# Expert down matrices loaded in pairs, 64 partitions to an expert, and multiplied on 64-row tiles: a two-layer decoder trunk on one core

## The reference

```python
for i in range(DEPTH):                      # 2 layers, 256 tokens, width 1024
    ...                                     # convolution, linear attention, latent attention, merged
    x = layer_norm(alpha * x + mix, ...)
    # mixture of experts: 8 groups of 8, best group, then its two best experts
    y = 0
    for each token t, for each of its two experts e:
        h = silu(x[t] @ w_gate[e]) * (x[t] @ w_up[e])      # 1024 -> 256
        y[t] += weight[t, e] * (h @ w_down[e])             # 256 -> 1024
    x = layer_norm(alpha * x + y, ...)
    ple = sigmoid(x @ w_ple_gate + b) * (p[i] @ w_ple_up)
    x = layer_norm(alpha * x + ple, ...)
```

## Time and profile before

| | |
|---|---|
| median of 3 runs | 1505.33 us (1503.81 to 1505.48) |
| profiled execution, its own time | 1503.91 us |
| its span | 1502.2 us |
| PE busy | 1259.2 us (84%) |
| DVE, ACT, POOL busy | 554.2, 207.2, 27.9 us |
| DMA moved | 503.85 MB, mean 335 GB/s |
| granted TensorE clock, mean | 0.924 of 2.4 GHz |

### The profile page before, as it was taken

One profiled execution on the slowest core, in us unless ns is written; L12 is line 12 of the kernel. 1 busy time (PEld: TensorE's weight loads), 2 busy tenths in 40 slices (PEclk: granted clock), 3 DMA queues, 4 the chain that ended last, 5 costly groups with the idle time before them and its releaser, 6 DMA issues.

```text
span 1502.2 us, 20998 instructions
## 1 busy us (share of the span) xinstructions
PE 1259.2 (84%) x8621; PEld 690.0 (46%) x8621; DVE 554.2 (37%) x987; ACT 207.2 (14%) x413; POOL 27.9 (2%) x90
## 2 busy tenths in 40 slices
PE   9999999986774777579999999999677568757797
PEld 5665444742342434235466554456334325423354
DVE  6677775510110111111667677754111101101126
ACT  2322000310100000000212220012111000000011
POOL 2000000000000000000100000000000000000000
PEclk9999999997888889889999999999888879888899
DMA  9644558899999999999955255679999999999992
GB/s 314 230 172 150 174 211 332 318 426 426 427 427 425 425 425 426 428 427 416 330 192 204 97 204 168 230 301 355 426 427 426 427 426 424 426 426 428 426 408 87
DMA packets 110537, 503.85 MB, mean 335 GB/s; under 512 B 13042, under 2 KB 16132, under 8 KB 62468
## 3 DMA queue, kind: packets, MB, share of 16 engines
q1 hardware_dynamic: 109876, 501.84, 83.3%
q10 hardware_dynamic: 592, 1.06, 0.2%
HBM read 501.83 MB, written 1.05 MB: 335 GB/s over the span
## 4 chain that ended last, share of the span: by engine, by line
PE 60%; DMA 36%; issue 1%; SPq 1%; DVE 1%; ACT 0%; POOL 0%; DVEq 0%; POOLq 0%
DMA scratch<-in_w_down 35%; PE ps L852 20%; PE ps L1497 11%; PE ps L901 6%; PE ps L1448 5%; PE ps L805 4%; PE ps L1429 2%; PE ps L1507 2%; PE ps L1615 1%; PE ps L1344 1%; PE ps L825 1%; SPq L553 1%; PE ps L1316 0%; DMA ring<-in_w_in 0%; PE ps L1367 0%
## 5 line engine op out<-in xcount | busy, mean ns | idle before, releaser
L1497 PE MATMUL ps<-ring,pads 128*32 128x512 f32 x384 | 161.6, 784 | 199.2 <-DMA scratch<-in_w_down 199.2
L1497 PEld LDWEIGHTS ps<-ring,pads 128*32 128x32 f32 x384 | 33.9, 139 | 300.6 <-DMA scratch<-in_w_down 162.3
L1448 PE MATMUL ps<-scratch,pads 128*32 128x256 f32 x1792 | 171.6, 379 | 0.0
L1448 PE MATMUL ps<-ring,pads 128*32 128x256 f32 x2304 | 171.4, 379 | 0.0
L852 PE MATMUL ps<-ring,scratch 128*128 128x512 f32 x384 | 169.2, 592 | 0.0
L1497 PE MATMUL ps<-scratch,pads 128*32 128x512 f32 x512 | 161.6, 790 | 0.0
L2657 DVE COPY mats<-ps 128x512 f32<-128x512 f32 x32 | 22.1, 691 | 349.3 <-PE ps L1497 349.3
L1429 PEld LDWEIGHTS ps<-pads,xT 128*128 128x128 f32 x960 | 114.8, 197 | 25.3 <-issue 25.3
L1429 PE MATMUL ps<-pads,xT 128*128 128x128 f32 x960 | 116.0, 280 | 10.6 <-issue 10.6
L1507 PE MATMUL ps<-mats,pads 128*128 128x512 f32 x256 | 118.8, 606 | 0.0
L1448 PEld LDWEIGHTS ps<-scratch,pads 128*32 128x32 f32 x1792 | 89.3, 110 | 58.9 <-issue 17.6
(11 more groups left out here) (364 smaller groups left out, 1314.3 us busy)
## 6 DMA issues: line engine op xcount, KB each, us to landing
ring<-in_w_up SPq DMA_DIRECT2D x28, 2048.0 KB, 32.5
scratch<-in_w_down SPq DMA_DIRECT2D x28, 2048.0 KB, 23.0
scratch<-in_w_gate SPq DMA_DIRECT2D x28, 2048.0 KB, 30.4
ring<-in_w_in SPq DMA_DIRECT2D x48, 1024.0 KB, 7.1
ring<-in_w_gate SPq DMA_DIRECT2D x12, 3072.0 KB, 31.8
scratch<-in_w_up SPq DMA_DIRECT2D x14, 2048.0 KB, 31.9
ring<-in_w_down SPq DMA_DIRECT2D x14, 2048.0 KB, 27.0
scratch<-in_w_gate SPq DMA_DIRECT2D x22, 1024.0 KB, 14.5
```

What stands on the lines that cost most here:

```text
L1448: ins = mm(ps[32 * j:32 * j + 32, 2, i * 256:i * 256 + 256], xgT[:, k, 32 * j:32 * j + 32], w[j][:, k, :], start=(k == 0), stop=(k == K - 1))
L1497: ins = mm(ps[32 * j:32 * j + 32, n, :], hT[:, cc, 32 * j:32 * j + 32], w[j][:, cc, n * 512:n * 512 + 512], start=(cc == 0), stop=(cc == 1 ...
```

## The change

- **Slots.** `w_down` of experts 0 and 1 of a turn, and of 2 and 3, now need two neighbouring slots. The ring and `x` become one tensor `ring_x`, in which `x` follows `r[11]`, and the order of slots in each layer is shifted so that the pairs are neighbours. In scratch memory the pair is EARLY+4 and EARLY+5; LATE, which was in it before, takes the gate matrix of expert 0 of the even turns, which was in EARLY+5.
- **Loads.** `load_down`: two experts are 512 rows of w_down; they are laid on 128 partitions with four neighbouring rows in each, 16 KB in one piece, so that the first expert has partitions 0 to 63 and the second 64 to 127. Where matrices are loaded singly (turn 0, half of turn 1), a load brings one half of the 16 KB of all partitions. The last turn keeps the layout of before.
- **Products.** The down product of an expert is four matmuls of 64 rows for each half of the columns, 32 matmuls in a turn. Experts 0 and 2 lie on rows 0 to 63 of the array, 1 and 3 on 64 to 127. For this `gate_up` puts the experts into strips in the order 0, 2, 1, 3 (`place_of`), the hidden values are taken in quarters (`hquarter`) and transposed by eight 64 x 64 products with the identity, and `weigh_P` permutes its columns in the same way.
- **Counting.** `ring_free` rises at other instructions for the down slots, since reads of a pair end together.

```diff
-    for end in (4, 8, 10, 12):
+    for end in (4, 8):
...
+    for n in (8, 10):
+        assert slots[n + 1] - slots[n] == 1 or (slots[n], slots[n + 1]) == (RING - 1, XSLOT)
+        runs.append((n, n + 2))
     return runs
+
+
+def place_of(j):
+    return 2 * (j % 2) + j // 2
...
-    order, last, landings, over_landings, layers = list(range(RING)), {}, {}, {}, []
+    order, last, landings, over_landings, layers = [(i - MOE0) % RING for i in range(RING)], {}, {}, {}, []
...
-        gate = [[EARLY + 5, r[0], r[1], r[2]], [EARLY + 1, EARLY + 2, MERGED, SIG]]
+        gate = [[LATE, r[0], r[1], r[2]], [EARLY + 1, EARLY + 2, MERGED, SIG]]
         up = [[r[3], r[4], EARLY, EARLY + 3], r[7:11]]
-        down = [[r[5], r[6], EARLY + 4, LATE], [r[11], XSLOT, EARLY + 4, LATE]]
+        down = [[r[5], r[6], EARLY + 4, EARLY + 5], [r[11], XSLOT, EARLY + 4, EARLY + 5]]
...
-        slots += [r[0], r[1], r[2], r[3], r[4], r[5], r[7], r[8], r[9]]
+        slots += r[0:9]
...
-        order = [r[10], r[11], r[6], r[0], r[1], r[2], r[3], r[4], r[5], r[7], r[8], r[9]]
+        order = r[9:12] + r[0:9]
...
+                def load_down(s, n, count, experts, arrived, step=None, skipped=0):
...
+                        src = a["w_down"][bass.ds(experts[n0 % 4], 2), :, :].rearrange("e (p c) n -> (e p) (c n)", c=4)
+                        dst = double_ap(L, s, n0)
+                        if count == 1:
+                            half = slice(SLOT * (n - n0), SLOT * (n - n0) + SLOT)
+                            src, dst = src[:, half], dst[:, half]
+                    sp.dma_start(dst, src).then_inc(arrived[leader_of(L, s, n)], 16)
...
-                    for cc in range(2):
+                    if not parted:
+                        alone(pe)
+                    for cc in range(0 if parted else 4):
+                        for r in (slice(0, 64), slice(64, 128)):
+                            ins = mm(ps[r, 3, 64 * cc:64 * cc + 64], hquarter[r, cc, :], ident[r, r],
+                                     start=True, stop=True, skip_group_check=True)
...
-                        w = [slot_of(s, 8 + j, arrived, count, step).rearrange("p (c n) -> p c n", c=2) for j in range(4)]
-                        order = [(n, cc) for n in range(2) for cc in range(2)]
+                        for n0 in (8, 10):
+                            slot_of(s, n0, arrived, count, step)
+                        alone(pe)
+                        pairs = [double_ap(L, s, n0).rearrange("p (c n) -> p c n", c=4) for n0 in (8, 10)]
+                        for n in range(2):
+                            for cc in range(4):
+                                for j in range(4):
+                                    r = slice(64 * (j % 2), 64 * (j % 2) + 64)
+                                    o = 32 * place_of(j)
+                                    ins = mm(ps[o:o + 32, n, :], hT_pair[r, cc, 32 * (j // 2):32 * (j // 2) + 32],
+                                             pairs[j // 2][r, cc, n * 512:n * 512 + 512], start=(cc == 0), stop=(cc == 3),
+                                             skip_group_check=True)
```

More of the change, by code:

```diff
@@ L102, in split_runs @@
     runs, n = [], 0
-    for end in (4, 8, 10, 12):
+    for end in (4, 8):
         while n < end:
             m, step = n + 1, None
-            while m < end and XSLOT not in (slots[m - 1], slots[m]) and (slots[m] < RING) == (slots[n] < RING):
+            while m < end and (slots[m] < RING) == (slots[n] < RING):
                 d = slots[m] - slots[m - 1]
@@ L445, in slot_ap @@
             if i == XSLOT:
-                return x.rearrange("p t d -> p (t d)")
+                return ring_x[:, RING, :]
             o = slot0 + SLOT * (i - RING)
@@ L604, in load @@
                     alone(sp)
-                    src = w[bass.ds(experts[n % 4], count), :, :]
-                    src = src.rearrange("e (p k) n -> p e (k n)", k=K if n < 8 else 2)
+                    src = w[bass.ds(experts[n % 4], count), :, :].rearrange("e (p k) n -> p e (k n)", k=K)
                     sp.dma_start(run_ap(PLAN[L]["slots"][q:q + count]), src).then_inc(arrived[leader_of(L, s, n)], 16)
+                def load_down(s, n, count, experts, arrived, step=None, skipped=0):
+                    q, n0 = MOE0 + 12 * s + n, run_of(L, s, n)[0]
+                    if loaded_singly(s, n) and PLAN[L]["prev"][q] is None:
+                        wait_slot(q, L)
+                    else:
+                        written = slice(q, q + 1) if step is None and count == 1 else slice(q - n + n0, q - n + n0 + 2)
+                        last_reader = max(PLAN[L]["prev"][written]) + 1 - skipped
+                        sp.wait_ge(ring_free, last_reader if step is None else step + last_reader)
+                    alone(sp)
+                    if step is not None and count == 1:
+                        half_rows = slice(64 * (n % 2), 64 * (n % 2) + 64)
+                        src = a["w_down"][bass.ds(experts[n % 4], 1), :, :].rearrange("e (p c) n -> (e p) (c n)", c=4)
+                        dst = double_ap(L, s, n0)[half_rows, :]
+                    else:
+                        src = a["w_down"][bass.ds(experts[n0 % 4], 2), :, :].rearrange("e (p c) n -> (e p) (c n)", c=4)
[4 more added lines that the diff above has]
+                    sp.dma_start(dst, src).then_inc(arrived[leader_of(L, s, n)], 16)
                 def load_part(m, part, g=None, skipped=0):
@@ L617, in load_part @@
                         n0, n1 = run_of(L, s, n)
+                        load_run = load if n < 8 else load_down
                         if loaded_singly(s, n):
-                            load(s, n, 1, experts, landed, None, skipped)
+                            load_run(s, n, 1, experts, landed, None, skipped)
                         elif n == n0:
-                            load(s, n, n1 - n0, experts, landed, None if g is None else g * 24, skipped)
+                            load_run(s, n, n1 - n0, experts, landed, None if g is None else g * 24, skipped)
                 def load_gate_by_halves(m):
@@ L671, in _ @@
                             for n in range(12):
-                                load(MID + uu, n, 1, [e + L * NE for e in es], over_landed, g * 24)
+                                (load if n < 8 else load_down)(MID + uu, n, 1, [e + L * NE for e in es], over_landed, g * 24)
                     load_part(MID, GATE_UP)
@@ L1461, in gate_up, with hidden_transposes @@
                     ins.then_inc(h_full, 1)
-                def hidden_transposes(c):
+                def hidden_transposes(c, parted=False):
                     pe.wait_ge(h_ready, c)
-                    for cc in range(2):
+                    if not parted:
[4 more added lines that the diff above has]
+                                     start=True, stop=True, skip_group_check=True)
+                            if cc == 0 and r.start == 0:
+                                ins.then_inc(ring_free, 1)
+                    for cc in range(2 if parted else 0):
                         ins = pe.transpose(ps[:, 3, 128 * cc:128 * cc + 128], hperm[:, cc, :], ident[:, :])
@@ L1486, in down @@
                     else:
-                        w = [slot_of(s, 8 + j, arrived, count, step).rearrange("p (c n) -> p c n", c=2) for j in range(4)]
-                        order = [(n, cc) for n in range(2) for cc in range(2)]
+                        for n0 in (8, 10):
[10 more added lines that the diff above has]
+                                             skip_group_check=True)
+                                    if n == 1 and cc == 3 and j == 2:
+                                        ins.then_inc(ring_free, 2)
+                            ins.then_inc((y_low, y_full)[n], 1)
+                        order = []
                     for n, cc in order:
@@ L1578, in section @@
                     keep_clock(idle, IDLE["last hidden"] if ends else 0)
-                    hidden_transposes(c0 + MID)
+                    hidden_transposes(c0 + MID, ends)
                     keep_clock(idle, IDLE["last weights"] if ends else 0)
```

41 lines of the change are left out of this document (25 added, 16 removed).

## The result

| | before | after |
|---|---|---|
| median | 1503.81 us (1502.56 to 1505.48, 5 runs) | 1538.59 us (1537.42 to 1539.18, 5 runs) |
| profiled span | 1502.2 us | 1535.7 us |
| PE busy | 1259.2 us (84%) | 1381.3 us (90%) |
| DMA moved, mean | 503.85 MB, 335 GB/s | 503.92 MB, 328 GB/s |

A forecast was written before the change was run, and what follows sets the result against it. Bytes were taken to bound the MoE's middle, stream holes its start, TensorE its tail. Terms +16.8 + 2 x 6.9 + 2 x 0.5 - 2 x 1.2 = +29.2 on 1503.91 us gave 1533.1 us; range 1515 to 1545.

The forecast's parts named there:

- the case: Forecast's main case, given 75%: all its terms hold, about 1533 us, with its own range of 1521 to 1542.
- late start: Start of each MoE: first gate load waits until about 240 us, eight loads behind; 9.1 and 7.7 us, sum +16.8.
- row pieces in the tail: Down products 13 and 14 of each layer: sixteen steps for eight, 3.44 us more each, +6.9 us a layer.
- transposes in the tail: Hidden values in each tail: two 128x128 transposes become eight 64x64 products, +0.5 us a layer.
- 16 KB rows: w_down loads: longer rows save a fixed 6 ns per row, 0.1 us a turn, -1.2 us a layer.
- The rival in which the wait is over early: Start of each MoE: LATE's slot is released well before 240 us, no late-start cost, 1516 us; 9%.
- The rival in which the row halves exclude each other: Down product: both halves write one PSUM bank and take turns, 32 steps, 13.8 us; 1576 us in all; 13%.
- The wait of a turn: Middle of the MoE: TensorE's idle time before each down product shrinks from 8.7 to 4.8 us.
- the wait of 5 us keeps the low clock: Before product 13: clock still falls in the shorter wait, so 6.9 us a layer stands, not 5.2 and 4.3.
- part 2: Down product on 64-row tiles: 16 matmuls a turn become 32, hidden in the middle, +6.9 us a layer in the tail.
- so the stream does not run dry: Middle turns: SP load behind the down product is issued 3.4 us later, with about 23 us until its landing.

The follow-up runs named there:

- b1: Kernel before with LATE and EARLY+5 exchanged in the slot table, nothing else: 1521.81 us (ratio 1.0122).
- b2: Kernel before with every down product but a layer's last computed twice on 128 rows, 64 records each: 1518.13 us (ratio 1.0095).
- a2: Changed kernel with each load of a pair issued as two, rows of 8 KB, same layout: 1539.53 us (ratio 1.024).
- a3: Changed kernel with 128 semaphore increments ahead of TensorE's first instruction, shifting its later program: 1550.44 us (ratio 1.031).
- a1: Changed kernel with the turn 0 gate matrix for LATE issued behind the other seven gate and up matrices: 1518.77 us (ratio 1.0101).
- b4: Kernel before with LATE and EARLY+5 exchanged and the down products computed twice: 1535.15 us (ratio 1.0206).
- b5: Kernel before with 26 idle identity products, meant for product 13 but placed ahead of product 14, which has no wait: 1515.16 us (ratio 1.0072).
- a4: Changed kernel with 16 idle identity products ahead of the down product of turns 1, 3, 5, 9, 11, 13: 1532.83 us (ratio 1.0194).
- b3: Kernel before with the third down matrix of turn 0 issued ahead of the first two: 1504.38 us (ratio 1.0000).
- b6: Kernel before with 26 idle identity products ahead of the down product of turns 1, 3, 5, 9, 11, 13: 1503.70 us (ratio 0.9997).

## Why the prediction was right

The direction and the case were the forecast's; 1538.6 lies inside the range and inside the forecast's own 1521 to 1542, 5.5 us above the worked-out 1533.1.

| step | predicted | shown |
|---|---|---|
| late start | +16.8 | +16.8 of span (b1); +8.8 and +7.9 by product 13, predicted 9.1 and 7.7 |
| row pieces in the tail | +13.8 | +14.0 (b2); in after 4.68 + 3.43 and 2.33 + 3.43 = +13.9 |
| transposes in the tail | +1.0 | +0.9 (1.70 against 1.27 us) |
| 16 KB rows | -2.4 | -2.1 of span (a2); -0.9 by medians |
| hole at mid-layer | none | +3.4 by windows, +2.8 by a3 |
| sum | +29.2 | +32.9; span +33.5 |

The agreement to a tenth of a microsecond is luck. The spans are those of single executions, and the runs of one kernel differ by 1.2 to 4.6 us; by the medians b1 is 18.7 and b2 15.0 us over the kernel before. What the runs bear out is the mechanism of each term and its size within some 2 us.

**Late start.** 4.5 and 5.1 MB of later holes were counted as filled, and at 417 GB/s they were (in layer 1, 413 GB/s from 999.2 to 1053.6 us). The time of release was bounded at 240.3 us from the earlier trace rows; it was 239.6. The rival in which the wait is over early falls with this row: a1 and b1 both have it at 240.

**Down product.** 7.00 us at full clock is the 3.57 + 3.44 of the prediction to the hundredth. The rival in which the row halves exclude each other falls. One phrase of the prediction is off without changing the number: the array does not stay 4 of 8 tiles wide. Before, four matmuls of 128 rows in four strips took all of it; now the four pieces of a step take half of it, which is why the steps double. The timeline of after, at half clock:

```profile
352.20 1.06 PE L1541 MATMUL ps<-ring_x,pads 64*32 64x512 f32 x2 [5.01 <-DMA scratch<-in_w_down]
352.22 1.06 PE L1541 MATMUL ps<-scratch,pads 64*32 64x512 f32 x2
353.03 1.09 PE L1541 MATMUL ps<-ring_x,pads 64*32 64x512 f32 x2
353.07 1.07 PE L1541 MATMUL ps<-scratch,pads 64*32 64x512 f32 x2
```

The four records of a step, of two experts on each row half and all into one bank, begin within 0.04 us of each other; sixteen steps make the 64 records of 9.10 us. This is against the Trainium skill (TensorEngine Tiling (Array Packing), "Gotcha 1: PSUM Pressure"), by whose rule the product would have taken an estimated 13.8 us, 32 steps of 0.43 us; the measurement decides. The wait of a turn is 4 to 5 us, as forecast, except ahead of turn 7, where no gather stands before it and it is 8.3 and 9.5 us.

That the wait of 5 us keeps the low clock was also right: in the earlier trace rows a step at half clock is 0.86 us, in the timeline above 0.83 to 0.85. TensorE fell to half speed in a wait of 5.01 us just as in one of 8.54. Product 13 of layer 1 was 2.3 us longer than before and that of layer 0 4.7, since the clock came back after different numbers of steps. That the sum over the layers is what the term said is luck: in the six kernels with 64 records that had such a wait and no idle products, product 13 took from 8.49 to 9.92 us.

**Rows of 16 KB** gained 0.1 us a turn, as worked out, and one row is one packet. The fixed cost of 6 ns a row that the sum took from the earlier trace rows fits the turns (0.09 us over 16 rows); the Trainium skill's 3 cycles (DMA: Bandwidth & Descriptors, "Why small descriptors are slow"), an estimated 3.5 ns, would have given -1.4 us, which the runs do not tell apart from -2.1, with 0.9 us between the medians.

**The step that was missing** is in part 2: "so the stream does not run dry". It holds for each ordinary turn, and it was said of all. At mid-layer the loop's end and the branch hold TensorE for 5.3 us, a second stop of 0.8 or 3.6 us came, and the product of turn 7 is 2.8 and 2.7 us longer (8.43 and 9.14 us, before 5.62 and 6.43). Of these only the branch was in the earlier trace rows. The runs show that neither alone is enough: b2 and b4 have the long product and no second stop, and no hole; b5 has a second stop (2.60 us) and the short product, and its stream ran on. Together they empty the queue. The late start has some part in it: a1, with the same products and stops of 0.95 and 3.65 us, has a hole in layer 1 alone, of 1.6 us. Of the 5.5 us between the predicted 1533.1 and the median 1538.6, about 3 are this hole, 1.2 are the median's distance from the profiled execution's own 1537.4, and the rest are the small terms.

**Still open:** how much of the program TensorE has at hand behind the branch, which would say where a second stop falls; where a4 lost what its filled holes should have given back; and most of the 0.6 us between the sum of the table and the span (the gate and up products of the tail are 0.1 us longer each, 7.04 against 6.91 in the earlier trace rows).

## What to carry to other kernels

When a layout change forces buffers to swap roles, follow the first load into each and list what stands behind it in that queue: one waiting load held back 8.4 MB for 36 us and cost more than the doubling of the matmuls. A matmul on 64 rows took as long as one on 128, so splitting the contraction pays only if the other row half gets work of its own at the same time; here four experts filled the four column strips before and after, and half the height gave the same time for a step and twice the steps. And price room by its worst turn, not its usual one: 5 us of room in the ordinary turn hid the fact that there was none at the branch.

## What the runs showed of the hardware that was not expected

- 128 semaphore increments in a row on TensorE's queue took 18.5 us, 0.14 us each, at the program's start.
- Behind the branch that passes over the turns of the overfull experts, TensorE stood for 5.05 to 5.63 us in every kernel, and in some a second time inside the next gather: 0.77 and 3.63 us in after, 0.95 and 3.65 in a1, 1.11 and 3.95 in a2, 2.60 in layer 1 of b5, and not in before, b1, b2, b3, b4, b6, a3 and a4. Each second stop ended 1.3 to 1.6 us after a 16 KB packet of the program had landed.
- Two 64-row halves writing to different partitions of one PSUM bank ran side by side at full speed, 0.43 us a step of four.
- TensorE's clock fell to half in waits of 4 to 5 us. 16 products of the identity in such a wait kept it at 2.4 GHz and made a product of 9.92 us one of 7.07. With 3.04 us of a wait left behind such products (b6, turn 3), it fell within the product.
